# Two transformer blocks with product-key experts on one core: the last score unit of each expert stage in row order

## What is computed

```
def peer_ffn(h, w_pq, sub_keys, expert_u, expert_v):
    q = (h @ w_pq).reshape(B, S, PEER_HEADS, 2, PEER_DQ // 2)
    scores = einsum('bshpd,hpkd->bshpk', q, sub_keys)
    ...                        # the 16 best of 16 x 16 candidates per head: expert_idx, gate
    u = take(expert_u, ic)     # 1024 features per expert
    a = einsum('cd,chkd->chk', hc, u)
    w = gc * gelu(a)
    return einsum('chk,chkd->cd', w, take(expert_v, ic))
```

## Time and profile before

| | value |
|---|---|
| median of three runs | 2804.44 us |
| the profiled execution | 2806.19 us, its span 2804.4 us |
| granted clock of TensorE, mean | 0.991 of full speed |
| VectorE busy | 2110.9 us, 75% |
| ScalarE busy | 1391.5 us, 50% |
| DMA | 537.41 MB, 54.1% of the 16 engines' span |

### The profile page before, as it was taken

How to read it: one execution, slowest core, us unless ns; L and a number is a source line. 1 busy time by engine, 2 the same in 40 slices (tenths; PEclk the granted TensorE clock), 3 DMA queues, 4 the chain that set the end, 5 groups by cost and what they waited for, 6 DMA issues and landing times.

```text
span 2804.4 us, 39919 instructions
## 1 busy us (share of the span) xinstructions
PE 2734.0 (97%) x16374; PEld 2332.6 (83%) x16374; DVE 2110.9 (75%) x3134; ACT 1391.5 (50%) x1630; POOL 211.3 (8%) x172
## 2 busy tenths in 40 slices
PE   7999999999999999999999999999999999999998
PEld 6778888788888888888878888897888888888887
DVE  7777887765555589998889955546699989799655
ACT  4645446554465455554444344565555544434443
POOL 0210002000023001200000000030012100000000
PEclk8999999999999999999999999999999999999999
DMA  8757866455554345554554555543455544455554
GB/s 311 263 195 302 314 239 239 159 195 199 191 186 149 131 172 195 183 179 170 175 178 170 180 194 192 209 147 136 166 180 195 181 168 170 159 195 175 186 195 143
DMA packets 76069, 537.41 MB, mean 192 GB/s; under 512 B 8560, under 2 KB 8944, under 8 KB 12656
## 3 DMA queue, kind: packets, MB, share of 16 engines
q1 hardware_dynamic: 75888, 534.86, 54.1%
HBM read 527.48 MB, written 7.34 MB: 191 GB/s over the span
## 4 chain that ended last, share of the span: by engine, by line
PE 66%; issue 22%; DVE 7%; ACT 3%; DMA 2%; POOL 1%; SPq 0%; POOLq 0%; DVEq 0%; ACTq 0%
PE banks L453 18%; PE banks L461 9%; PE banks L531 7%; PE banks L533 7%; PE banks L541 7%; DVE wlo L1531 3%; PE banks L505 2%; PE banks L507 2%; PE banks L516 2%; ACT whi L1026 2%; PE banks L475 1%; PE banks L477 1%; PE banks L487 1%; PE banks L971 1%; PE banks L571 1%
## 5 line engine op out<-in xcount | busy, mean ns | idle before, releaser
L1026 ACT ACTIVATE whi<-raw 128x2048 fp32r<-128x2048 f32 x438 | 839.1, 1916 | 988.5 <-issue 788.0
L1531 DVE TENSOR_TENSOR wlo<-raw,whi 128x2048 fp32r<-128x2048 f32 x438 | 1011.3, 2309 | 281.8 <-ACT whi L1026 281.4
L453 PE MATMUL banks<-ht,whi 128*128 128x512 f32 x2880 | 703.8, 394 | 5.4 <-DVE big L1629 2.9
L453 PEld LDWEIGHTS banks<-ht,whi 128*128 128x128 f32 x2880 | 527.9, 189 | 109.1 <-issue 3.6
L531 PE MATMUL banks<-whi,ht 128*128 128x512 f32 x1152 | 460.6, 400 | 16.1 <-DVE ht L1619 9.1
L533 PE MATMUL banks<-whi,ht 128*128 128x512 f32 x1152 | 453.9, 394 | 0.0
L461 PEld LDWEIGHTS banks<-ht,wlo 128*128 128x128 f32 x2880 | 369.1, 191 | 14.6
L461 PE MATMUL banks<-ht,wlo 128*128 128x256 f32 x2880 | 373.3, 282 | 0.0
L541 PE MATMUL banks<-wlo,ht 128*128 128x512 f32 x1152 | 287.8, 389 | 2.1 <-DVE wlo L1531 2.1
L531 PEld LDWEIGHTS banks<-whi,ht 128*128 128x128 f32 x1152 | 219.3, 190 | 62.2 <-issue 17.7
L533 PEld LDWEIGHTS banks<-whi,ht 128*128 128x128 f32 x1152 | 219.2, 190 | 44.3
(11 more groups left out here) (277 smaller groups left out, 3331.7 us busy)
## 6 DMA issues: line engine op xcount, KB each, us to landing
raw<-in_pu SPq DMA_DIRECT2D x128, 1024.0 KB, 4.9
raw<-in_pv SPq DMA_DIRECT2D x128, 1024.0 KB, 4.9
raw<-in_win SPq DMA_DIRECT2D x52, 1024.0 KB, 4.9
big<-in_wmod SPq DMA_DIRECT2D x28, 1024.0 KB, 6.8
raw<-in_wgate SPq DMA_DIRECT2D x22, 1024.0 KB, 5.1
raw<-in_wup SPq DMA_DIRECT2D x22, 1024.0 KB, 5.7
raw<-in_wdown SPq DMA_DIRECT2D x22, 1024.0 KB, 5.1
raw<-in_wmod SPq DMA_DIRECT2D x20, 1024.0 KB, 4.9
```

Of the source, the lines that this page charges most:

```text
L453: m = e.matmul(bank[b + n], h[:, q, c[n]], M.both[:, q * 512:(q + 1) * 512], start=q == 0, stop=False, skip_group_check=True)
L1026: e.activation(whi(j), slot[u][0], ACT.Copy).then_inc(*hi.mark(j))
L1531: e.tensor_tensor(wlo(j), slot[u][0], whi(j).bitcast(F32), ALU.subtract).then_inc(*lo.mark(j))
```

## The change

The last score unit of each layer (u = 63) is computed in another order, and two things that follow it are moved.

- `wide_unit_by_rows` runs over q outside. For each row it issues two high matmuls (n = 0 and 1) and then two low ones. It waits for `lo` before its first matmul. `hi_read` comes with the last high matmul, in row 7. After rows 1 and 3 it raises a new signal, `row_free`.
- On ScalarE the splits of v = 0 and v = 1 wait for `row_free` of row 1 and row 3 instead of the end of unit 63, and stand side by side after the gelu of unit 62.
- The `whi` of the second value tile, which stood before this gelu, now comes after both splits and before the copy of unit 63.

The lists of VectorE, GpSimd and SyncE are as they were.

```
+        def wide_unit_by_rows(key, M, free):
+            k = take()
+            b, held = banks.pair(key)
+            ...
+            for n in range(2):
+                evicted(held[n])
+            on.wait_ge(*lo.at(k))
+            for q in range(8):
+                for n in range(2):
+                    m = e.matmul(bank[b + n], h[:, q, c[n]], M.both[:, q * 512:(q + 1) * 512], start=q == 0, stop=False,
+                                 skip_group_check=True)
+                if q == 7:
+                    m.then_inc(*hi_read.mark(k))
+                for n in range(2):
+                    m = e.matmul(bank[b + n][:, 0:256], w[:, q, c[n]], M.hi[:, q], start=False, stop=q == 7,
+                                 skip_group_check=True)
+                if q in free:
+                    m.then_inc(*row_free.mark((*key[1:], q)))
+            m.then_inc(*unit.mark(k))
...
-                if u:
+                if u == 63:
+                    wide_unit_by_rows(("a", l, u), HT, (1, 3))
+                elif u:
                     wide_unit(("a", l, u), HT, ready, between)
...
-                    on.wait_ge(*unit.at(mm1 if v < 2 else mm1 + v - 1))
+                    if v < 2:
+                        on.wait_ge(*row_free.at((l, 63, 2 * v + 1)))
+                    else:
+                        on.wait_ge(*unit.at(mm1 + v - 1))
...
                 k = take()
-                upto(k + 2)
+                if u < 63:
+                    upto(k + 2)
                 gelu(u - 1)
                 if u == 63:
                     mm1 = k
                     split_weights(0)
+                    split_weights(1)
+                    upto(k + 2)
                 region(on, l, u)
                 apart(ag(u * 512, 512), ("a", l, u), k)
-            split_weights(1)
             gelu(63)
```

More of the change, by code:

```diff
@@ L323, in program @@
     d_out = [signal(f"out{i}", 16) for i in range(4)]
-    unit, hi_read, turned, scored, valued, modsum, gated = (signal(x) for x in (
-        "pe_unit", "pe_hi_read", "pe_turned", "pe_scored", "pe_valued", "pe_modsum", "pe_gated"))
+    unit, hi_read, turned, scored, valued, modsum, gated, row_free = (signal(x) for x in (
+        "pe_unit", "pe_hi_read", "pe_turned", "pe_scored", "pe_valued", "pe_modsum", "pe_gated", "pe_row_free"))
     hi, took_a, squared, part_hi, a_set, a_soft = (signal(x) for x in (
@@ L464, in wide_unit @@
             return k
+        def wide_unit_by_rows(key, M, free):
+            k = take()
+            b, held = banks.pair(key)
+            h, w = whi(k).rearrange("p (k n) -> p k n", k=8), wlo(k).rearrange("p (k n) -> p k n", k=8)
+            c = [slice(n * 128, (n + 1) * 128) for n in range(2)]
+            for n in range(2):
[13 more added lines that the diff above has]
+            m.then_inc(*unit.mark(k))
         def a_unit(key, M, ready, between=None, b=None, head=False, low=None):
```

## The result

| | before | changed |
|---|---|---|
| median of ten timed runs | 2803.91 us | 2797.95 us |
| lowest and highest | 2800.75, 2806.40 | 2795.14, 2801.93 |
| the profiled execution | 2806.19 | 2798.75, its span 2797.0 |
| mean granted clock in it | 0.991 | 0.993 |

The changed kernel is 6.0 us faster by the medians. The ratio of the times is 0.998, 95% interval 0.9972 to 0.9989, which is 3.1 to 7.9 us. The forecast gain of 4.7 us lies in it; the forecast time of 2799.7 is 1.75 us too high.

The account below looks back on a forecast made before the run. TensorE, busy 97%, was taken to bound the kernel, waiting 2.0 us at each layer's seam from scores to values. Two seams at 2.37 us won give 4.7, so 2804.44 - 4.7 = 2799.7 us, range 2797.3 to 2804.0.

Parts of the forecast that it names:

- Unit 63 takes 5.57: TensorE, last score unit: 32 matmuls in row order take 5.57 us as before, alternating 512 and 256 columns costing nothing.
- Splits, and value unit 0 without a wait: ScalarE's splits start at 1416.03 and 1416.55, value unit 0 is released at 1417.51; TensorE's 2.00 us wait goes.
- The copy 0.63 late, the sum 0.49 late: Unit 63's ScalarE copy, behind the waiting `whi`, comes 0.63 us later; VectorE's sum and everything behind it 0.49 later.
- Value unit 1 at 12.63, unit 2 at 19.54: TensorE starts value unit 1 at 1424.93, 3.24 us earlier, and value unit 2 at 1431.84, 2.37 us earlier.
- VectorE is late next: At value unit 2 TensorE waits 0.87 us for VectorE's low split; VectorE's queue keeps back 1.24 of 3.61 us.
- The clock falls because of the idle time and the new waits don't cost it: Clock fall after the 2.00 us seam wait costs 1.61 us; new waits of about 0.5 and 0.87 leave it up.
- The signs of being wrong: Wrong if value unit 1 starts over 7.3 us after unit 63's issue ends, or value unit 2 over 14.2.
- What is won stays: Behind value unit 2 VectorE's cycle is 5.64 against TensorE's 6.04, so the wait doesn't recur and 2.37 us stay.
- The ceiling of 3.61 us per seam: Each step from scores to values costs 2.00 us waiting plus 1.61 at lower clock; two cost 7.2 us.
- the first rival: The whole seam comes back because VectorE has less work or more slack: 7.2 us, 2797.2 us; chance 0.12.
- the rival in which the clock takes part of the gain: Not all earlier seams lost their clock (2802.8 us), or the new waits cost it (2801.2 or 2802.9); chance 0.20.

Follow-up runs that it names:

- all units in rows: Changed kernel with all score units but the first in row order, gate groups moved behind row 3; 2813.80 us, ratio to before 1.0039.
- copy-first kernel: Changed kernel with unit 63's copy ahead of the second value tile's high part on ScalarE; 2795.64 us, ratio to before 0.9974; again 2795.32, 0.9972.
- late products: Changed kernel with VectorE's two products of groups 0 and 1 behind the low split of value unit 2 and following low weights; 2798.43 us, ratio to before 0.9981.
- filler: Kernel before with 8 extra high matmuls in TensorE's wait ahead of value unit 0 at each seam; 2800.88 us, ratio to before 0.9993.
- one early split: Changed kernel with only the split of v = 0 early, that of v = 1 back behind unit 63's copy; 2797.40 us, ratio to before 0.9983.

## Why the prediction was right

**Point by point**, each against the changed kernel's profile, from the start of unit 63:

- *Unit 63 takes 5.57.* It took 5.58. The alternation costs 0.01 at most, and the kernel with all units in rows agrees.
- *Splits, and value unit 0 without a wait.* Forecast for the first split 3.73 (1416.03 - 1412.30), measured 3.75; value unit 0 at 5.57, measured 5.58.
- *The copy 0.63 late, the sum 0.49 late.* Forecast copy at 7.39 and sum at 7.98, measured 7.41 and 8.01.
- *Value unit 1 at 12.63, unit 2 at 19.54.* Measured 12.66 and 19.57, with waits of 0.29 and 0.70 in the brackets (the bracket counts from the end of the last matmul, not from when the next could have been issued). The gain at value unit 2 is 21.91 - 19.57 = 2.34, forecast 2.37.
- *VectorE is late next.* Shown by the copy-first kernel, which moved its chain by 1.62 and ended the wait, and by the late products, which moved the wait by a unit.
- *The clock falls because of the idle time and the new waits don't cost it.* The first half was shown by the filler. The second half holds for all of the changed kernel's seams seen, four in two profiles, and two more with one early split.
- *The signs of being wrong.* Value unit 1 started 12.66 - 5.58 = 7.08 us behind unit 63 (at most 7.3 was allowed), value unit 2 13.99 (14.2).
- *What is won stays.* 983.95 us between the seams against 983.88, and 2797.0 - 2434.00 = 363.0 us behind the second against 2804.4 - 2441.43 = 363.0.

**What was not right.** Three things.

The ceiling of 3.61 us per seam was too low. It took the bracket of 2.00 us for the wait, and the bracket counts from the end of the last matmul; from where the next could have been issued it is 7.72 - 5.57 = 2.15. Copy first gained 3.87 and 3.82, more than the ceiling, and so the first rival's price was near 7.7 us and not 7.2. The forecast itself does not use the ceiling; it subtracts places. What VectorE's queue kept back was 3.87 - 2.34 = 1.53, where the prediction had 1.24.

The forecast took a fall of the clock at each seam of the kernel before. Seven of eight had one, so the seams are worth (7 x 2.34 + 1 x 0.71) / 8 = 2.1 each, 4.3 us in the mean, and the rival in which the clock takes part of the gain was true for one seam.

The other deviation goes the other way: the measured gains are 6.0 and 5.6. What lies above 4.3 to 4.7 is not at the seams. The profiles say where it lies in them. The four of the kernel before have a mean span of 2801.5 us, the three with the changed kernel's places (two of it, one of one early split) 2795.8, 5.7 less: 4.2 at the seams, 1.1 between them, 0.4 ahead of the first and nothing behind the second. The 1.1 is the fall near 1991, which three of the four have, at 1.5 us each, and none of the three. The timed runs point the same way: the mean granted clock is 0.9915 in the 54 runs of the kernel before that stand beside the experiments, and 0.9930 in 21 of the changed kernel. That is 4.2 us less lost to the clock, and the falls at the seams make up only 7/8 x 2 x 3.4 x 0.5 = 3.0 of it. So the excess looks like falls elsewhere in the program. That the change makes them rarer is not shown: both profiles of copy first have the fall near 1991. As far as falls are drawn by chance, it was luck that 2797.95 still lay in the range, whose lower edge is 2797.3; whether it is chance stays open.

## What to carry to other kernels

An idle engine has two prices where its clock depends on its work: here 2.0 us of waiting were followed by 3.4 us at half speed, which cost 1.6 us more, and filling the wait with useless matmuls won 1.7 us per seam although value unit 0 started only 0.08 earlier. When a producer is released early, follow the queue of every engine behind it to the second and third consumer: here the first wait went in full, and a copy queued behind a tile that had become later held back 1.5 of the 3.9 us per seam until the two were swapped. Releasing a buffer piece by piece is cheap if the pieces cost nothing to make, but the thing that used to be released in the middle of the unit is now released at its end; done once at the seam that was paid back by one reordering, done in every unit it brought some 5 us of waits in the first layer's score units and at the seam behind them.

## What the runs showed of the hardware that was not expected

- TensorE's stream of 512-column and 256-column float32 matmuls with a full weight load for each runs at 0.228 and 0.12 us apart in both orders tried: grouped 5.57, alternating in pairs 5.57 to 5.58 us for 32.
- After the same 2.00 us of idle time the clock was 0.50 for 3.4 us in seven seams of eight, and 1.00 in the eighth. After a wait of 1.49 us in the stage before it stayed at 1.00; at another place, near 1991, a wait of 1.49 or 1.50 us was followed by a fall in three of four profiles of the kernel before and in none of two of the changed one.
- The runs of the kernel before spread over 2797.4 to 2808.6 us (32 runs on one chip). The timeline from one seam to the next is the same to 0.1 us apart from such falls, so the position of an instruction after a fixed start told more here than the median time did.
